# Between the first mixer and the experts: output product, norms, router and choice by token tile; gates, lists and second bias behind the first gather

## The reference, cut to what matters

```
mod = silu(c) @ w_ada + b_ada                      # six rows of 1024: sh1, sc1, gt1, sh2, sc2, gt2
x = x + gt1 * rms_norm(concat(att, gla) @ w_out, g_post_mix)
h = rms_norm(x, g_pre_ffn) * (1 + sc2) + sh2
logits = h @ w_router + b_router                   # 32 experts
top_v, top_i = top_k(logits, 4); gates = softmax(top_v)
for each expert e, for its tokens:
    u = h @ w_mlp1[e] + b_mlp1[e]                  # 1024 x 2048, glu and linear columns interleaved
    a = min(u_glu, 7) * sigmoid(1.702 * ...) * (clip(u_lin, -7, 7) + 1)
    y += gate * (a @ w_mlp2[e] + b_mlp2[e])        # 1024 x 1024
x = x + gt2 * rms_norm(y, g_post_ffn)
```

## Time and profile before

| | us |
|---|---|
| median of 3 runs (1800.9 to 1804.72) | 1804.32 |
| the profiled execution | 1804.44 |
| its span, first to last instruction | 1801.2 |
| TensorE busy with matmuls | 1693.1 (94%) |
| weight loads of TensorE | 917.6 (51%) |
| VectorE busy | 715.1 (40%) |
| ScalarE busy | 497.0 (28%) |

### The profile page before, as it was taken

How to read it: one execution, slowest core, us unless ns; L and a number is a source line. 1 busy time by engine, 2 the same in 40 slices (tenths; PEclk the granted TensorE clock), 3 DMA queues, 4 the chain that set the end, 5 groups by cost and what they waited for, 6 DMA issues and landing times.

```text
span 1801.2 us, 21172 instructions
## 1 busy us (share of the span) xinstructions
PE 1693.1 (94%) x8277; PEld 917.6 (51%) x8277; DVE 715.1 (40%) x1017; ACT 497.0 (28%) x700; POOL 22.7 (1%) x50
## 2 busy tenths in 40 slices
PE   5987689999999999999999999997999999999998
PEld 2853423333333333333333333335888797788886
DVE  2643531222212122221212121216666656766665
ACT  2542211212111121211111111204333444453333
POOL 1000100000000000000000000000000000000000
PEclk8996789999999999999999999998999999999999
DMA  9646849999999999999999999996655563446551
GB/s 353 236 190 261 312 190 426 429 428 430 427 429 428 428 430 427 430 428 428 430 428 429 428 428 430 427 428 204 208 188 183 177 201 119 164 153 201 188 181 69
DMA packets 111207, 575.11 MB, mean 319 GB/s; under 512 B 6960, under 2 KB 61296, under 8 KB 81728
## 3 DMA queue, kind: packets, MB, share of 16 engines
q1 hardware_dynamic: 108320, 564.22, 78.1%
q0 software_dynamic: 2512, 9.28, 1.6%
q10 hardware_dynamic: 336, 1.07, 0.1%
HBM read 573.50 MB, written 1.05 MB: 319 GB/s over the span
## 4 chain that ended last, share of the span: by engine, by line
PE 63%; DMA 27%; DVE 7%; issue 1%; ACT 1%; SPq 0%; DVEq 0%; ACTq 0%
DMA ring<-in_w_mlp 24%; PE PS L957 17%; PE PS L648 9%; PE PS L1008 8%; PE PS L944 7%; PE PS L1037 6%; PE PS L1010 4%; DMA ring<-in_w_ada 2%; PE PS L685 2%; PE PS L937 1%; PE PS L862 1%; PE PS L905 1%; DMA ring<-in_w_out 1%; PE PS L922 1%; DVE scr L1945 1%
## 5 line engine op out<-in xcount | busy, mean ns | idle before, releaser
L957 PE MATMUL PS<-ring,scr 128*64 128x512 f32 x2176 | 500.9, 614 | 9.1 <-DMA ring<-in_w_mlp 9.0
L957 PEld LDWEIGHTS PS<-ring,scr 128*64 128x64 f32 x2176 | 149.0, 134 | 342.1 <-issue 312.0
L944 PE MATMUL PS<-ring,scr 128*64 128x512 f32 x1088 | 248.5, 598 | 0.0
L1975 DVE TENSOR_TENSOR w_lo<-ring,w_hi 128x2048 fp32r<-128x2048 f32 x90 | 206.0, 2289 | 79.9 <-ACT w_hi L1442 79.8
L1442 ACT ACTIVATE w_hi<-ring 128x2048 fp32r<-128x2048 f32 x90 | 172.5, 1917 | 236.1 <-PE PS L1010 132.1
L1008 PE MATMUL PS<-HT_both,w_hi 128*128 128x512 f32 x640 | 227.0, 399 | 0.0
L1933 DVE TENSOR_SCALAR scr<-iota,scr 128x128 f32<-128x128 f32 (+1 forms) x68 | 20.5, 344 | 414.4 <-PE PS L957 414.4
L1944 DVE TENSOR_SCALAR scr<-PS 64x512 f32<-64x512 f32 x68 | 46.4, 683 | 336.7 <-PE PS L957 335.6
L1010 PE MATMUL PS<-HT_both,w_lo 128*128 128x256 f32 x640 | 179.7, 281 | 0.0
L1391 ACT ACTIVATE scr<-scr 64x512 f32<-64x512 f32 x68 | 42.3, 623 | 493.4 <-DVE scr L1944 493.4
L944 PEld LDWEIGHTS PS<-ring,scr 128*64 128x64 f32 x1088 | 71.9, 136 | 148.1 <-issue 148.1
(11 more groups left out here) (347 smaller groups left out, 1773.6 us busy)
## 6 DMA issues: line engine op xcount, KB each, us to landing
ring<-in_w_mlp SPq DMA_DIRECT2D x204, 2048.0 KB, 21.7
ring<-in_w_ada SPq DMA_DIRECT2D x24, 1024.0 KB, 9.3
ring<-in_ffn_w_gate SPq DMA_DIRECT2D x22, 1024.0 KB, 5.3
ring<-in_ffn_w_up SPq DMA_DIRECT2D x22, 1024.0 KB, 5.3
ring<-in_ffn_w_down SPq DMA_DIRECT2D x22, 1024.0 KB, 4.8
ring<-in_w_in SPq DMA_DIRECT2D x19, 1024.0 KB, 5.6
ring<-in_w_out SPq DMA_DIRECT2D x8, 1024.0 KB, 5.3
ring<-in_w_gate SPq DMA_DIRECT2D x8, 1024.0 KB, 5.0
```

The costliest lines, as they stand in the source:

```text
L944: mm = pe.matmul(PS[c * CAP:(c + 1) * CAP, 6, :], aT[:, h, k, :], w[:, k, c * HALF:(c + 1) * HALF], start=(h == 0 and k == 0), stop=(h == ...
L957: mm = pe.matmul(PS[c * CAP:(c + 1) * CAP, 4 + h, :], xsT[:, 2 * (j % 2) + k, j // 2, :], w[:, k, h, c, :], start=False, stop=(j == 3 and ...
L1975: dve.tensor_tensor(w_lo[:, at % PAIRS, :], raw(n), w_hi[:, at % PAIRS, :].bitcast(F32), ALU.subtract).then_inc(lo_ready, 1)
```

## The change

Four things are done in another order or in other pieces, with the same arithmetic.

- The output product of tile 0 is finished before that of tile 1. Both norms go in half rows of 512, tile 0 while TensorE is still at tile 1; squares go to `dump`, the gain is multiplied in before the root is known, and the root's table is loaded ahead (`warm`).
- Router and choice go by tile. The eight comparisons are one instruction for each tile. Counts and ranks follow the choice at once, and `sel` and `eh`, which release the first gather, come right after the ranks.
- The split of the first bias, the gates, the list of overflow passes and `GT` come behind that release. The clears of `selgT` and `ys` are gone.
- Pass 0 is written out before the loop (`opening=True`): behind chunk 1 it transposes the gates, and where other passes scatter it starts the sum with the second bias. `b1` has moved in `scr`.

```diff
-b1 = cut(2 * D, at=1776)
+b1 = cut(2 * D, at=6576)
...
+dump = cut(D, at=1792)
...
     for g in range(4):
         pool.dma_start(b1[g * E:(g + 1) * E, :], a["b_mlp1"][0]).then_inc(load_moe, 16)
     pool.dma_start(b2, a["b_mlp2"][0]).then_inc(load_moe, 16)
+    pool.wait_ge(mix_h, 2 * TT)
     for m, g in ((1, "ffn1_norm_2"), (2, "mix_norm_2")):
         pool.dma_start(gains[:, m, :], row(a[g][0])).then_inc(load_gains2, 16)
     pool.dma_start(wsr, a["gmlp_w_s_2"][0].rearrange("g i j -> i g j")).then_inc(load_mix2, 16)
...
+    def out_tile(j, t):
+        hi, lo = split(in1("out", j), 2)
+        for k in range(2):
+            x_hi, x_lo = [x[:, 2 * j + k, t * P:(t + 1) * P] for x in mix]
+            for x, w in ((x_hi, hi), (x_hi, lo), (x_lo, hi)):
+                for h in range(2):
+                    mm = pe.matmul(PS[:, 2 * t + h, :], x, w[:, k, h * HALF:(h + 1) * HALF],
+                                   start=(j == 2 and k == 0 and x is x_hi and w is hi),
+                                   stop=(j == 1 and k == 1 and x is x_lo))
+        return mm
+    out_tile(2, 0)
+    pe.wait_ge(s_olo, 2)
+    out_tile(2, 1).then_inc(weights_used, 1)
+    ada_sum(3)
+    out_tile(3, 0)
+    out_tile(3, 1).then_inc(weights_used, 1)
+    ada_sum(4)
+    out_tile(0, 0)
+    ada_sum(5)
+    out_tile(1, 0).then_inc(mix_done, 1)
+    out_tile(0, 1).then_inc(weights_used, 1)
+    out_tile(1, 1).then_inc(weights_used, 1)
+    def turn_mixed(t):
+        for hf in range(2):
+            pe.wait_ge(mix_h, 2 * t + hf + 1)
+            turn_half(t, hf)
+    def logits(t, copied):
+        for k in range(KC):
+            if k % 4 == 0:
+                pe.wait_ge(*copied[k // 4])
+            mm = pe.matmul(PS[:, t, 0:E], HT[:, k, t * P:(t + 1) * P], wr[:, k, :], start=(k == 0), stop=(k == KC - 1))
+        mm.then_inc(r_lg, 1)
+    turn_mixed(0)
+    pe.wait_ge(load_wr, 16)
+    logits(0, ((turn_act, 1), (turn_dve, 1)))
+    turn_mixed(1)
+    logits(1, ((turn_act, 2), (turn_act, 3)))
+    pe.wait_ge(r_sel, 1)
+    pe.matmul(PS[:, 5, 0:E], before[:], Sel[:, 0, :], start=True, stop=True)
+    pe.matmul(PS[:, 5, E:2 * E], ones[:], Sel[:, 0, :], start=False, stop=False, skip_group_check=True)
+    pe.wait_ge(r_sel, 2)
+    pe.matmul(PS[:, 5, E:2 * E], before[:], Sel[:, 1, :], start=False, stop=True, skip_group_check=True).then_inc(r_pe, 1)
+    for t in range(TT):
+        mm = pe.matmul(PS[:, 6, 0:E], ones[:], Sel[:, t, :], start=(t == 0), stop=(t == 1))
+    mm.then_inc(r_pe, 1)
+    def turn_gates():
+        pe.wait_ge(r_dve, R_G)
         for t in range(TT):
+            mm = pe.transpose(PS[0:E, 3, t * P:(t + 1) * P], G[:, t, :], ident[:])
+        mm.then_inc(r_pe, 1)
+    def second_bias(t):
+        pe.wait_ge(r_act, 2)
         for h in range(2):
             pe.matmul(PS[:, 2 * t + h, :], GT[:, t * P:(t + 1) * P], b2[:, h * HALF:(h + 1) * HALF],
                       start=True, stop=False, skip_group_check=True)
...
+            if opening and j == 1:
+                turn_gates()
         pe.wait_ge(s.sel, i + 2)
         gather(s)
-        pe.wait_ge(s.ys, i + 1)
-        scatter((0,))
+        if opening:
+            second_bias(0)
+        else:
+            pe.wait_ge(s.ys, i + 1)
+            scatter((0,))
         turn_hidden(0, 6)
-        scatter((1,))
+        if opening:
+            second_bias(1)
+        else:
+            scatter((1,))
...
+    pe.wait_ge(bias_lo, 2)
+    pe.wait_ge(load_moe, 5 * 16)
+    expert_pass(main, 0, opening=True)
+    with pe.Fori(1, E) as i:
         expert_pass(main, i)
...
+    def mixed_copy(t, hf):
+        act.wait_ge(turn_ps, 4 + 2 * t + hf + 1)
+        act.activation(HT[:, 4 * hf:4 * hf + 4, t * P:(t + 1) * P], bank4(4 + 2 * t + hf), ACT.Copy).then_inc(turn_act, 1)
+    def mixed_squares(t):
+        for hf in range(2):
+            if hf:
+                act.wait_ge(mix_w, t + 1)
+            act.activation(dump[:, hf * HALF:(hf + 1) * HALF], PS[:, 2 * t + hf, :], ACT.Square, scale=D ** -0.5,
+                           accum_out=msq[:, t, hf:hf + 1]).then_inc(sq_ready, 1)
+    def added_squares(t):
+        for hf in range(2):
+            cols = slice(hf * HALF, (hf + 1) * HALF)
+            act.wait_ge(mix_x, 2 * t + hf + 1)
+            act.activation(dump[:, cols], X[:, t, cols], ACT.Square, scale=D ** -0.5,
+                           accum_out=msq[:, t, hf:hf + 1]).then_inc(sq_ready, 1)
+    def mixed_root(n):
+        act.wait_ge(var_ready, TT + n)
+        act.activation(ss[:, (n - 1) // 2:(n + 1) // 2], ss[:, (n - 1) // 2:(n + 1) // 2], ACT.Sqrt).then_inc(std_ready, 1)
...
+    warm(ACT.Sqrt)
+    act.wait_ge(mix_done, 1)
+    mixed_squares(0)
+    mixed_root(1)
+    added_squares(0)
+    mixed_root(2)
     act.wait_ge(weights_used, N_MIX1)
+    mixed_squares(1)
+    mixed_root(3)
+    mixed_copy(0, 0)
+    added_squares(1)
+    mixed_root(4)
+    warm(ACT.Exp)
+    mixed_copy(1, 0)
+    mixed_copy(1, 1)
+    act.wait_ge(load_moe, 5 * 16)
     for c in range(2):
         rows = slice(c * CAP, (c + 1) * CAP)
...
+    act.wait_ge(r_pe, 3)
+    act.activation(GT, PS[0:E, 3, 0:S], ACT.Copy).then_inc(r_act, 1)
...
-    for m in range(3, 6):
-        ada(m)
+    dve.wait_ge(load_gains1, 3 * 16)
+    dve.wait_ge(ada_ev, 2)
+    dve.tensor_tensor(gains[:, 1, :], gains[:, 1, :], mod[:, 2, :], ALU.mult)
+    ada(3)
+    dve.memset(G, 0.0)
+    dve.memset(rk, 0.0)
+    dve.memset(row_of, 0.0)
+    ada(4)
+    dve.wait_ge(ada_ev, 6)
+    link(dve.scalar_tensor_tensor(out=gains[:, 2, :], in0=mod[:, 4, :], scalar=1.0, in1=gains[:, 2, :],
+                                  op0=ALU.add, op1=ALU.mult))
+    dve.tensor_reduce(row_of[:, 0:E], ident[:].rearrange("p (g e) -> p e g", g=4), AX.X, ALU.add)
+    ada(5)
     dve.wait_ge(ada_ev, 8)
     link(dve.tensor_tensor(gains[:, 3, :], gains[:, 3, :], mod[:, 5, :], ALU.mult))
+    def mixed_mean(t):
+        dve.tensor_scalar(ss[:, t:t + 1], msq[:, t, 0:1], msq[:, t, 1:2], EPS, ALU.add, ALU.add).then_inc(var_ready, 1)
+    def weigh_mixed(t):
+        weigh = lambda hf: dve.tensor_tensor(hcol(H[:, t], hf), PS[:, 2 * t + hf, :], hcol(gains[:, 1], hf), ALU.mult)
+        weigh(1).then_inc(mix_w, 1)
+        dve.wait_ge(sq_ready, TT + 4 * t + 1)
+        weigh(0)
+        dve.wait_ge(sq_ready, TT + 4 * t + 2)
+        mixed_mean(t)
+    def mixed_inverse(n):
+        dve.wait_ge(std_ready, TT + n)
+        st_n = ss[:, (n - 1) // 2:(n + 1) // 2]
+        link(dve.reciprocal(st_n, st_n))
+    def add_mixed(t):
+        for hf in range(2):
+            x = hcol(X[:, t], hf)
+            dve.scalar_tensor_tensor(out=x, in0=hcol(H[:, t], hf), scalar=ss[:, t:t + 1], in1=x,
+                                     op0=ALU.mult, op1=ALU.add).then_inc(mix_x, 1)
+        for hf in range(2):
+            dve.wait_ge(mix_x, 2 * t + hf + 1)
+            dve.tensor_tensor(hcol(H[:, t], hf), hcol(X[:, t], hf), hcol(gains[:, 2], hf), ALU.mult)
+            if hf == 0:
+                dve.wait_ge(sq_ready, TT + 4 * t + 4)
+                mixed_mean(t)
+    def shift_mixed(t):
+        for hf in range(2):
+            h = hcol(H[:, t], hf)
+            dve.scalar_tensor_tensor(out=h, in0=h, scalar=ss[:, t:t + 1], in1=hcol(mod[:, 3], hf),
+                                     op0=ALU.mult, op1=ALU.add).then_inc(mix_h, 1)
+    dve.wait_ge(mix_done, 1)
+    weigh_mixed(0)
+    mixed_inverse(1)
+    add_mixed(0)
+    mixed_inverse(2)
+    shift_mixed(0)
+    dve.wait_ge(weights_used, N_MIX1)
+    weigh_mixed(1)
+    dve.wait_ge(turn_ps, 6)
+    dve.tensor_copy(HT[:, 4:8, 0:P], bank4(5)).then_inc(turn_dve, 1)
+    mixed_inverse(3)
+    add_mixed(1)
+    mixed_inverse(4)
+    shift_mixed(1)
+    def choose(t):
+        dve.wait_ge(r_lg, t + 1)
+        link(dve.tensor_tensor(lg[:, t, :], PS[:, t, 0:E], brt, ALU.add))
+        link(dve.max(top8[:, t, :], lg[:, t, :]))
+        dve.tensor_scalar(ssum[:, t:t + 1], top8[:, t, 0:1], -1.0, None, ALU.mult).then_inc(r_neg, 1)
+        link(dve.max_index(idxu[:, t, :], top8[:, t, :], lg[:, t, :]))
+        link(dve.tensor_copy(idxf[:, t, :], idxu[:, t, :]))
+        link(dve.tensor_tensor(oh[:, t], iota[:, 0:E].unsqueeze(1).to_broadcast([P, TOPK, E]),
+                               idxf[:, t, 0:TOPK].unsqueeze(2).to_broadcast([P, TOPK, E]), ALU.is_equal))
+        dve.tensor_reduce(Sel[:, t, :], oh[:, t].rearrange("p k e -> p e k"), AX.X, ALU.add).then_inc(r_sel, 1)
+    choose(0)
+    choose(1)
+    dve.wait_ge(r_sel, TT)
     dve.wait_ge(r_pe, 1)
+    link(dve.scalar_tensor_tensor(out=rk[:, :, 0:E], in0=PS[:, 5, 0:TT * E].rearrange("p (t e) -> p t e", t=TT),
+                                  scalar=1.0, in1=Sel, op0=ALU.add, op1=ALU.mult))
+    link(dve.tensor_scalar(rk, rk, -1.0, None, ALU.add))
     for t in range(TT):
+        dve.tensor_scalar(sel[:, t, :], iota[:, 0:CAP], rk[:, t, 0:1], None, ALU.is_equal)
+    dve.tensor_scalar(eh[:], halves, row_of[:, 0:1], None, ALU.mult).then_inc(main.sel, 1)
```

(53 more changed lines are left out.)

103 lines of the change are left out of this document (10 added, 93 removed).

## The result

The changed kernel takes 1780.23 us (median of 4 runs, 1778.89 to 1780.76) against 1804.09 for the kernel before: a ratio of 0.9866, 95% interval 0.9854 to 0.9878. It is 23.9 us faster, where 24.0 were forecast. Its profiled execution took 1780.10 us with a span of 1778.2, so 24.3 and 23.0 less than before.

The account below looks back on a forecast made before the run. Expert weight transfers bound the kernel, their engines idle 23.9 us until TensorE's first expert product. Gather 26.8 us earlier, less 1.45 (pass 0 work) and 1.4 (clock), gains 24.0: 1804.4 to 1780.4 us, range 1777.5 to 1787.

Parts of the forecast that it names:

- Tile 0's h done: Norm of tile 0 in half rows: starts at 188.95, takes 7.0 us, done at 195.95.
- Gates and second bias in pass 0: Pass 0 gets gate transposes and second bias in place of two scatters: together 1.45 us longer.
- The clock: Start of pass 0, after idle: part of it runs at half speed, costing 1.4 us, bounds 0 and 3.4.
- A delay in pass 0 counts in full: Pass 0: delays hit the weight stream, since chunk 4's reload already landed 0.6 us later than a full stream's.
- The sum: Whole change: 26.8 us from the earlier gather, less 1.45 and 1.4 in pass 0, gives 24.0.
- with twice that time: Start of pass 0: a clock rise taking twice as long after the bias row would cost 3.4 us.
- chunk 4's reload: Pass 0: slot free at 267.6, 9.2 us to landing, 0.6 us later than a full stream.
- Rival (c): Weight stream full, no clock cost, bias loads out of the way: gain 25.8 to 26.5, or 1778 us; chance 0.12.
- Rival (a): Pass 0 later through clock, choice, hand-offs and select: gain 19.2, or 1785 us, up to 1790; chance 0.22.
- Rival (b): Expert loop: transfers swallow the gain and TensorE just waits, leaving 1804 us; chance 0.02.
- Rival (d): Clock does not rise in pass 0: a whole pass at 1.2 GHz, 28 us longer, or 1807 us; chance 0.03.
- GpSimd's select: Select over the spatial weights moves to about 220 and meets the list: charged 0, 0.8 us in the upper bound.

Follow-up runs that it names:

- 128-row kernel: Changed kernel with the second bias contracted over 128 rows instead of 32, gates zero-padded, bias rows loaded four times: 1779.12 us, ratio 0.9862.
- product by chunk: Changed kernel with the output product back in the old order by chunk, norms starting when all of it is done: 1788.81 us, ratio 0.9916.
- last part alone: Kernel before, with only gates, list and splits moved behind the gather's release and second bias in pass 0: 1795.3 us, ratio 0.9954.
- bias in pass 16: Changed kernel with the second bias added in pass 16 instead of pass 0, VectorE zeroing the banks first: 1780.83 us, ratio 0.9872.
- bias twice: Changed kernel with the second bias computed twice in pass 0, four more matmuls, same result: 1788.84 us, ratio 0.991.
- the two kernels with the filling: Changed kernel with seven unread matmuls in TensorE's idle time before the gather: 1779.17 us; the same plus second bias over 128 rows: 1777.49 us.
- the undone parts: Changed kernel with one part reversed each: output product by chunk 1788.81 us, router in one piece 1784.0, bias split before the gather's release 1787.02.
- the kernel with the idle time filled: Changed kernel with seven unread matmuls in TensorE's idle time between tile 0's transposes and the gather: 1779.17 us, ratio 0.9863.
- the last-pass kernel: Changed kernel with the second bias added once in pass 31 instead of pass 0, VectorE zeroing the banks first: 1780.93 us, ratio 0.9872.

## Why the prediction was right

Point by point, predicted against the changed kernel's profile:

- Tile 0's h done: 195.95 against 195.98. The first is partly luck: tile 0's product ended 0.3 later than reckoned and the norm was 0.3 shorter (6.7 for 7.0). Tile 1's: 203.15 against 202.8. Router's end: 208.05 against 207.62. The choice: 1.6 against 1.75 (207.62 to 209.38). Gather: 211.4 against 211.32. First product: 217.9 against 217.92. The cut of a chain into pieces of 0.6 to 0.8 us from rows held, since nearly all links are existing operations of half the length.
- Gates and second bias in pass 0: 1.45 predicted. The 128-row kernel, which has no fall of the clock, shows them at 30.5 - 28.6 = 1.9. Each tile's share is 1.91 and not 1.8, so tile 0's adds 0.5 (0.4 reckoned) and tile 1's 0.9 (0.75); the two gate transposes are 0.32, with 0.1 more for the product that they cut in two. This term was too small by 0.5.
- The clock: 1.4 predicted, 1.65 measured (5.23 - 3.58), but not where I put it. At the start of pass 0 it was up (0.99 from 215 on), which was my lower bound of 0 there; it fell behind the second bias, which I had not considered. The forecast of this term was right in size by luck. Of the other kernels, three pay in both places (product by chunk, last part alone, bias in pass 16).
- "A delay in pass 0 counts in full": shown by the bias twice and by the table, with slope 1 from t0 + 50.
- The sum: pass 1 moved by 23.2, where 24.0 were forecast; the two terms above account for the difference (0.5 and 0.25). The stream's end moved by 22.3; the span by 23.0; the time by 24.3, of which 1.3 lie outside the span. The last 1.0 to 1.3 either way are not explained and are the size by which executions differ.
- Small slips of the working, which decide nothing: the stretches of the earlier trace rows put the clock's fall at 198.2 and its rise at 242.6, not at 198.6 and 242.3; the half speed "with twice that time" costs 3.1, not 3.4 (217.1 + 7.0 - 217.9 = 6.2, halved); chunk 4's reload was 0.7 behind a full stream, not 0.6.
- Rival (c), the full stream, is real and was near: the two kernels with the filling reach it, at 1779.2 and 1777.5, where 1778 was named. The allowance I gave it, 25.8, is 24.9 in the table (1014.9 - 990.0).
- Rival (a) did not happen, but its kind is what the undone parts run into. Rival (b) falls: the engines have no idle stretch left. Rival (d) falls: the clock was low for 3.5 us of pass 0.
- GpSimd's select, charged at nothing, cost nothing, but not as reckoned: it was to meet the list at about 220, and its loads landed so late that it runs at 229.73, with no neighbour on VectorE. It takes 1.09 there instead of 1.88, and the bias splits are 2.47 for two, so 1.2 each, where one of them was 2.00. So both lost by the meeting. It was a meeting with both splits and not with one: the select began at 226.80, inside the first (226.50 to 227.72, not slowed), and ended at 228.68, inside the second. The trace agrees with the rule of the Trainium skill (SBUF — State Buffer, Who interferes with whom).

```profile
211.30 2.47 DVE L1956 TENSOR_TENSOR b1s<-scr,b1s 32x1024 fp32r<-32x1024 f32 x2
...
229.73 1.09 POOL L553 TENSOR_SCALAR_AFFINE_SELECT mod<-mod 128x1024 f32<-128x1024 f32 x1 [22.15 <-DMA mod<-in_gmlp_b_s]
```

## What to carry to other kernels

In a loop bound by transfers, what counts outside it is when the first buffer is released and how long the first pass holds the rest; find the gap in the transfer engines' share, and take no more from TensorE than closes it: with the gap closed, a pass 1 that started 1.6 us sooner still saw the stream end no sooner. Work moved into such a loop is hidden only by the difference between transfer and compute per pass times the passes left, here 0.75 us each, and work taken out may uncover a wait it stood in front of. Leave room for the clock in the price of an edit ahead of the loop or in its first pass: 3.8 us of added work cost 6.8 here, and a link made 2.5 us longer cost 6.8 in the median.

## What the runs showed of the hardware

- The granted clock falls to 1.2 GHz inside unbroken TensorE work too: behind the four second-bias matmuls of 32 rows (239 to 242.4 in the changed kernel, at a cost of 1.65 us), and in the kernel with the bias twice inside them, for 10 us. With the same matmuls over 128 rows it did not fall in either kernel profiled. It falls in some kernels and not in others with the same instructions around, so a single profile says little about it.
- Seven matmuls whose results nobody reads, 6.3 us of them, kept the clock at 2.4 GHz for the 17 us in which it was at 1.2 before. TensorE was busy 15.0 of these 17 us without them, at half the clock, and 15.5 with them; the first expert product came 3.2 us sooner.
- Behind a gap the stream ran below its full rate for a while: 362 GB/s from 250 to 260 in the changed kernel against 431 later, where the kernel with the idle time filled has 424. The gap alone is not shown to be the reason, since the 128-row kernel, with a share of 1.00 from 244 to 250, has 388 there.
- VectorE's and GpSimd's instructions slowed each other where they met: a bias split 2.00 us for 1.2, a select 1.88 for 1.09.
- Executions differ by up to 5 us already at t0 (193.7, in the last-pass kernel, to 198.8 in these profiles), which is more than most edits here are worth; only lengths counted from a common event tell them apart.
